# One more weight slot in an expert ring, and a reordered end of the routing, in a two-layer mixture-of-experts kernel

## The reference

```
def hier_moe(h, w_rg, b_rg, w_re, b_re, w_gate, w_up, w_down):
    x = h.reshape(-1, d)
    pg = softmax(x @ w_rg + b_rg)                       # 4 groups
    g_idx, g_prob = argmax(pg), max(pg)                 # the one group of a row
    el = (x @ w_re + b_re).reshape(-1, 4, 8)            # 8 experts in each group
    pe = softmax(el[chosen group])
    top_v, top_i = top_k(pe, 2)                         # two experts of a row
    top_v = top_v / sum(top_v)
    for every expert (g, e):
        hh = silu(x @ w_gate[g, e]) * (x @ w_up[g, e]) * gate[:, g, e]
        y = y + hh @ w_down[g, e]
    ...
hp = hp + yp                                            # mixer A in layer 0, B in layer 1
hp = hp + hier_moe(rms_norm(hp, norm_ffn[i]), ...)
```

## Time and profile before

| | |
|---|---|
| median of 3 runs | 1138.5 us (1138.3 to 1140.09) |
| the profiled execution | 1136.48 us, of which the span of the core's instructions is 1134.6 us |
| PE busy | 1009.6 us (89%), mean granted clock 0.952 |
| DVE, ACT, POOL busy | 421.5, 231.9, 254.0 us |
| DMA | 282.12 MB, mean 249 GB/s; in the expert stages about 417 GB/s |
| expert stage of layer 0 | from 253 us (first gather) to about 485 us |
| expert stage of layer 1 | from 866 us to about 1107 us |

### The profile page before, as it was taken

One profiled execution on the slowest core, in us unless ns is written; L12 is line 12 of the kernel. 1 busy time (PEld: TensorE's weight loads), 2 busy tenths in 40 slices (PEclk: granted clock), 3 DMA queues, 4 the chain that ended last, 5 costly groups with the idle time before them and its releaser, 6 DMA issues.

```text
span 1134.6 us, 17373 instructions
## 1 busy us (share of the span) xinstructions
PE 1009.6 (89%) x6608; PEld 715.2 (63%) x6608; DVE 421.5 (37%) x1367; ACT 231.9 (20%) x717; POOL 254.0 (22%) x408
## 2 busy tenths in 40 slices
PE   6999999978999989839899899999996999888980
PEld 5877777965555545438668687777895555555540
DVE  1234454342333322241242433435464333432326
ACT  4234442110000000033222332332311000000002
POOL 3612232011222221122121221212211122221223
PEclk9999999978999999969999999999996999999995
DMA  9412141569999999993320402227066999999996
GB/s 314 124 40 75 39 186 64 217 244 336 416 419 417 416 420 418 392 317 126 119 80 27 134 31 94 66 102 290 24 258 237 382 419 417 418 418 419 418 372 243
DMA packets 73333, 282.12 MB, mean 249 GB/s; under 512 B 10410, under 2 KB 37114, under 8 KB 47200
## 3 DMA queue, kind: packets, MB, share of 16 engines
q1 hardware_dynamic: 57520, 240.40, 53.9%
q0 software_dynamic: 14480, 31.65, 8.0%
q10 hardware_dynamic: 1248, 8.91, 2.0%
HBM read 268.66 MB, written 28.70 MB: 262 GB/s over the span
## 4 chain that ended last, share of the span: by engine, by line
PE 77%; DMA 13%; DVE 4%; issue 2%; ACT 2%; POOL 1%; SPq 1%; POOLq 0%; ACTq 0%; DVEq 0%
PE ps L1773 22%; PE ps L2075 16%; PE ps L1765 11%; DMA area<-in_w_up 8%; PE ps L2087 7%; PE ps L2060 2%; PE ps L2266 2%; PE ps L1749 2%; PE ps L2082 2%; PE ps L1836 2%; PE ps L1958 1%; PE ps L2232 1%; PE ps L1973 1%; PE ps L1988 1%; DMA area<-y_scratch 1%
## 5 line engine op out<-in xcount | busy, mean ns | idle before, releaser
L1773 PE MATMUL ps<-area 128*128 128x256 f32 x1152 | 266.4, 384 | 7.1 <-DMA area<-in_w_b_qkv 3.3
L2076 PE MATMUL ps<-area 128*64 128x256 f32 x1040 | 251.8, 398 | 0.0
L1773 PEld LDWEIGHTS ps<-area 128*128 128x128 f32 x1152 | 214.0, 191 | 37.9 <-issue 8.2
L2075 PE MATMUL ps<-area 128*64 128x256 f32 x912 | 220.7, 397 | 14.7 <-DMA area<-in_w_up 7.7
L2075 PEld LDWEIGHTS ps<-area 128*64 128x64 f32 x912 | 125.5, 143 | 80.2 <-issue 21.1
L2076 PEld LDWEIGHTS ps<-area 128*64 128x64 f32 x1040 | 143.0, 143 | 0.0
L675 POOL DMA_INDIRECT y_scratch<-area,idx_i x64 | 63.8, 997 | 352.2 <-DVE area L1490 302.3
L1765 PE MATMUL ps<-area 128*128 128x272 f32 x512 | 123.2, 395 | 0.0
L1475 DVE SCALAR_TENSOR_TENSOR area<-ps,area 64x256 f32<-64x256 f32 x64 | 31.4, 491 | 232.4 <-ACT area L966 232.4
L966 ACT ACTIVATE area<-ps,area 64x256 f32<-64x256 f32 x64 | 29.9, 468 | 412.5 <-PE ps L2076 412.5
L2087 PE MATMUL ps<-area 128*64 128x512 f32 x228 | 108.7, 599 | 1.1 <-DVE area L1483 0.8
(11 more groups left out here) (235 smaller groups left out, 1163.6 us busy)
## 6 DMA issues: line engine op xcount, KB each, us to landing
area<-in_w_up SPq DMA_DIRECT2D x65, 1024.0 KB, 24.6
area<-in_w_gate SPq DMA_DIRECT2D x57, 1024.0 KB, 23.0
area<-in_w_down SPq DMA_DIRECT2D x57, 1024.0 KB, 27.4
area<-in_w_b_qkv SPq DMA_DIRECT2D x12, 1024.0 KB, 8.5
hid<-in_w_down SPq DMA_DIRECT2D x8, 1024.0 KB, 24.5
hid<-in_w_gate SPq DMA_DIRECT2D x8, 1024.0 KB, 20.8
area<-y_scratch ACTq DMA_DIRECT2D x8, 1024.0 KB, 8.1
area<-in_w_a_qkv SPq DMA_DIRECT2D x6, 1024.0 KB, 13.0
```

Of the source, the lines that this page charges most:

```text
L1773: ins = nc.tensor.matmul(ps[:r, bank, at_col:at_col + F], x[:, k, COL[t]:COL[t] + r], w[:, k, :], start=k == k0, stop=k == k1 - 1)
L2075: nc.tensor.matmul(ps[0:CAP, bank, 0:F], x[:, k, :], wg[:, k, :], start=k == 0, stop=k == KD - 1)
L2076: ins = nc.tensor.matmul(ps[CAP:P, bank, 0:F], x[:, k, :], wu[:, k, :], start=k == 0, stop=k == KD - 1)
```

## The change

1. The ring has 22 slots in a new order. The new slot, M, lies where the routing's selection matrices are; it stands behind H1 and ahead of H0. It waits for the end of the mixer, for lists and counts (`r_slots`), and for a new semaphore `asked`, which POOL raises right behind the issue of gather 0. H1's wait for the landing of the gather is gone.
2. With the ring, the overfull block moves from expert 20 to expert 22 and its weights from load 64 to load 70.
3. `route_counts` takes three products (ones on `sofar`, ones on the last tile's two `hot`) in place of ten, and runs behind the last `route_slots`; it raises `r_slots` once more, and DVE waits for that ahead of `cnt`.
4. `route_before` does the product on `sofar` first and waits for `hot` only then.
5. The two copies of indices in `route_pick` are gone; the uint32 index is the scalar operand itself.
6. The routing's small tiles lie elsewhere; the overfull block's selection matrices have memory of their own. For a second and later overfull block a wait of DVE stands one step earlier.

```diff
-OV_AFTER = 20
+OV_AFTER = 22
...
-MOE_SLOTS = [["N0", "R4", "R5", "S0", "N1", "F5", "F6", "F0", "F1", "F2", "F3", "F4", "W0", "R0", "R1", "R2", "R3", "X0", "X1", "H1", "H0"]] * 2
+MOE_SLOTS = [["N0", "N1", "F5", "F6", "R4", "R5", "S0", "F0", "F1", "F2", "F3", "F4", "W0", "R0", "R1", "R2", "R3", "X0", "X1", "H1", "M", "H0"]] * 2
...
-    slot_at["S0"], slot_at["W0"] = R_S, 4864
+    slot_at["S0"], slot_at["W0"], slot_at["M"] = R_S, 4864, 6960
...
+        if name == "M":
+            return [(at[c, "o"], UNITS), (r_slots, 2 * layer + 2)]
...
-                    if name == "H1":
-                        sp.wait_ge(gath[0], 16 * (TWOS // XG * layer + 1))
+                    if name == "M":
+                        sp.wait_ge(asked, layer + 1)
                     load(key)
...
-            for j in range(XG):
+            gather(0)
+            pool.sem_inc(asked, 1)
+            for j in range(1, XG):
                 gather(j)
...
-                own(dve, nc.vector.tensor_copy(chosen[:r, t, 0:1], first_of[:r, t, 0, 0:1]))
-                own(dve, nc.vector.tensor_scalar(pen[:r, t, :], iota_e[:r, 0:G], chosen[:r, t, 0:1], -BIG,
+                own(dve, nc.vector.tensor_scalar(pen[:r, t, :], iota_e[:r, 0:G], first_of[:r, t, 0, 0:1], -BIG,
                                                  ALU.not_equal, ALU.mult))
...
-                own(dve, nc.vector.tensor_copy(chosen[:r, t, 1:3], first_of[:r, t, 1, 0:2]))
                 for c in range(2):
-                    ins = nc.vector.tensor_scalar(hot[c][:r, t, :], iota_e[:r, :], chosen[:r, t, 1 + c:2 + c], None,
+                    ins = nc.vector.tensor_scalar(hot[c][:r, t, :], iota_e[:r, :], first_of[:r, t, 1, c:c + 1], None,
                                                   ALU.is_equal)
...
-            dve.wait_ge(r_slots, layer + 1)
+            dve.wait_ge(r_slots, 2 * layer + 1)
...
+            dve.wait_ge(r_slots, 2 * layer + 2)
             own(dve, nc.vector.tensor_scalar(cnt, ps[0:1, 5, 0:NE], float(-CAP), None, ALU.add))
...
-            pe.wait_ge(r_hot, NT * layer + i + 1)
...
-            for c in range(2):
-                ins = nc.tensor.matmul(ps[:r, 4, 0:NE], before[:r, :r], hot[c][:r, t, :], start=c == 0, stop=c == 1 and i == 0)
             if i:
                 pe.wait_ge(r_sum, (NT - 1) * layer + i)
-                ins = nc.tensor.matmul(ps[:r, 4, 0:NE], ones[:, :r], sofar[:, i - 1, :], start=False, stop=True)
+                nc.tensor.matmul(ps[:r, 4, 0:NE], ones[:, :r], sofar[:, i - 1, :], start=True, stop=False)
+            pe.wait_ge(r_hot, NT * layer + i + 1)
+            for c in range(2):
+                ins = nc.tensor.matmul(ps[:r, 4, 0:NE], before[:r, :r], hot[c][:r, t, :], start=c == 0 and i == 0, stop=c == 1)
             ins.then_inc(r_before, 1)
...
         def route_counts(layer):
-            for i, t in enumerate(LATE):
-                r = ROWS[t]
-                for c in range(2):
-                    nc.tensor.matmul(ps[0:1, 5, 0:NE], ones[:r, 0:1], hot[c][:r, t, :], start=i == 0 and c == 0,
-                                           stop=i == NT - 1 and c == 1)
+            t = LATE[NT - 1]
+            nc.tensor.matmul(ps[0:1, 5, 0:NE], ones[:, 0:1], sofar[:, NT - 2, :], start=True, stop=False)
+            for c in range(2):
+                ins = nc.tensor.matmul(ps[0:1, 5, 0:NE], ones[:ROWS[t], 0:1], hot[c][:ROWS[t], t, :], start=False, stop=c == 1)
+            ins.then_inc(r_slots, 1)
...
         route_before(0, 4)
+        route_slots(0, 4)
         route_counts(0)
-        route_slots(0, 4)
```

More of the change, by code:

```diff
@@ L326, in program @@
     y2b = [part(2 * D * i, 2, D) for i in range(3)] + [part(R_X + 2 * D * i, 2, D) for i in range(2)]
[L327 to L334, removed]
-    hot = [h[:, :, 0:NE] for h in hot2]
[L336 to L350, removed]
+    assert 6 * D <= slot_at["M"] and 4 * D <= KD * N
+    R_T = 7232
+    sel = [part(R_T + 640 * i, NT, P) for i in range(2)]
+    both, sofar, em = (part(R_T + 1280 + 160 * i, NT, NE) for i in range(3))
+    stage_g, stage_e = part(R_T, 2, KD, G), part(R_T + 64, 2, KD, NE)
+    R_P = slot_at["M"] + SLOT
+    assert 6208 + 1024 <= R_T and R_T + 1280 + 3 * 160 <= R_P
+    hot2 = [part(R_P + 320 * i, NT, 2 * NE) for i in range(2)]
+    hot = [h[:, :, 0:NE] for h in hot2]
+    lg = part(R_P + 640, NT, NL)
+    gtop, etop = part(R_P + 840, NT, 8), part(R_P + 880, NT, 8)
+    where = part(R_P + 940, NT, 2)
+    pen = part(R_P + 950, NT, G)
+    rs = part(R_P + 970, 12, 8)
+    gexp = part(R_P + 1066, NT, G)
+    gw = part(R_P + 1086, 2, 8)
+    ovs = part(R_P + 1102, 128)
+    shifted = part(R_P + 1230, NT, 2)
+    root = part(R_P + 1240, NE)
+    idx_f = part(R_P + 1272, NE)
+    assert R_P + 1304 <= R_G
+    blocks = part(R_X + 2 * SLOT, NE * 8)
+    ov_at = [R_G + P * i for i in range(8)] + [R_F + 7 * SLOT + P * i for i in range(2)]
+    ov_sel = [[part(ov_at[NT * c + t], P) for t in range(NT)] for c in range(2)]
     first_of = sb("first_of", [P, NT, 2, 8], U32)
@@ L405, in program @@
     r_clear = sem("r_clear")
+    asked = sem("asked")
     ones = cst[:, C_ONE:C_ONE + P]
@@ L1430, in moe @@
             ins.then_inc(r_idx, 1)
-            own(dve, nc.vector.tensor_scalar(em[:, 0, :], ps[:, 3, 0:NE], -2.0, float(2 * KEY0), ALU.mult, ALU.add))
-            nc.vector.tensor_scalar(idx_i[:, 0, :], em[:, 0, :], cst[:, C_HALF:C_HALF + 1], None, ALU.add) \
+            own(dve, nc.vector.tensor_scalar(idx_f, ps[:, 3, 0:NE], -2.0, float(2 * KEY0), ALU.mult, ALU.add))
+            nc.vector.tensor_scalar(idx_i[:, 0, :], idx_f, cst[:, C_HALF:C_HALF + 1], None, ALU.add) \
                 .then_inc(r_idx, 1)
@@ L1523, in overfull_select @@
                     for c in range(2):
-                        ins = nc.vector.tensor_scalar(sel[c][:r, t, :].rearrange("p (a b) -> p a b", b=CAP), slot_no[:r], shifted[:r, t, c:c + 1],
+                        ins = nc.vector.tensor_scalar(ov_sel[c][t][:r, :].rearrange("p (a b) -> p a b", b=CAP), slot_no[:r], shifted[:r, t, c:c + 1],
                                                       cst[:r, (C_K1, C_K2)[c] + t:(C_K1, C_K2)[c] + t + 1],
@@ L1581, in moe @@
                     overfull_pick(o)
+                    wait_apart(dve, s["scat"], 16 * o)
                     overfull_select(o)
-                    wait_apart(dve, s["scat"], 16 * o)
                     overfull_rows(o)
@@ L2116, in overfull_list @@
                     for c in range(2):
-                        ins = nc.tensor.matmul(ps[:, 3, 0:2 * NE], sel[c][:r, t, :], hot2[c][:r, t, :],
+                        ins = nc.tensor.matmul(ps[:, 3, 0:2 * NE], ov_sel[c][t][:r, :], hot2[c][:r, t, :],
                                                start=t == 0 and c == 0, stop=t == NT - 1 and c == 1)
@@ L2334, in _ @@
         route_before(1, 4)
+        route_slots(1, 4)
         route_counts(1)
-        route_slots(1, 4)
         moe(1)
```

## The result

The changed kernel takes 1145.2 us (median) where the kernel before takes 1138.6: ratio 1.0047, 95% interval [1.0033, 1.0062]. It is slower by 5.4 us by the ratio (3.8 to 7.1) and by 6.6 between the medians; 4.1 us less were forecast, and 1137.7 was the upper end of the range. The profiled execution of after took 1145.5 us, with a span of 1143.7, 9.1 us more than the one of before. That is more than the ratio says, because the profiled execution of before (1136.48 us) was faster than each of the 13 runs of before, and that of after was close to the median.

What follows compares the result with a forecast made beforehand. Weight traffic was taken to bound layer 0, PE layer 1. Layer 0: 2.5 + 0.96 - 0.3 = 3.2; layer 1: 0.96 - 1.1 + 1.0 = 0.9; together 4.1 us off, median 1134.4 us, range 1130.3 to 1137.7.

Steps and rivals of the forecast that it cites:

- when `asked` comes: Start of layer 0's experts: the semaphore rises after POOL's 1.31 us for gather 0, at 254.6 less the routing's gain.
- what the first gather pays: Start of each expert stage: gather 0 lands later beside H1, by 0.3 us in layer 0 and 1.1 in layer 1.
- M's data come behind the gather's: Start of layer 0's experts: M's traffic follows gather 0's; 0.3 us (0 to 2.2) was taken for the gather's delay.
- they hardly meet: Start of layer 0's experts: H1's traffic, to about 254.5, and gather 0's data scarcely overlap; 0.3 us taken.
- The prediction's own sign of being wrong: Start of the expert stages: the prediction is wrong if gather 0 takes above 6 us.
- PE's start is late by the whole of it: Start of each expert stage, claimed if gather 0 takes 9.3 us: PE starts 4.3 us late in each layer.
- rival 3: First gather, both layers: it takes the later gathers' 9.3 us; together 5.1 us slower, 1143.6 us; chance 0.07.
- here it is one: First gather: the 9.3 us median stands behind some ten loads in the queue, here behind only one.
- the slot: Weight queue: 22 loads in before the first refill; layer 0 2.5 us earlier, layer 1 nothing in the time.
- the routing: Mixer's end, last tile: copies gone, products reordered; 0.96 us less for each layer, bounds 0.39 and 0.96.
- the block: Layer 1's overfull block: PE's stall of 2.3 us shrinks by 1.0, DVE's copy next late; bounds 0 and 2.3.
- The clock: After layer 1's block stall: granted clock 0.70 over 5.7 us, a loss of 1.7; gain counted 0, upper bound 1.7.

Runs made afterwards that it cites:

- run 2: The changed kernel with `asked` raised by a small POOL memset behind gather 0 instead of a plain increment; ratio 0.9972 [0.9951, 0.9993] to the kernel before.
- run 1: The changed kernel with M (and H0 behind it) held until gather 0 has landed, H1 still early; ratio 0.9973 [0.9954, 0.9993] to before, median 1138.8 us.
- the kernel of 3: The changed kernel with H1, M and H0 all behind gather 0's landing; ratio 0.9938 [0.9915, 0.9960] to before, 0.9958 in a repeat.
- run 5: The kernel before with the overfull block alone moved from expert 20 to 22, ring of 21; ratio 1.0002 [0.9983, 1.0021] to before.

## Why the prediction was wrong, step by step

- **Failed: when `asked` comes.** "Gather 0 is issued at 253.28 and takes POOL 1.31 us, so `asked` comes at 254.6." The sum laid the increment behind the gather's 1.31 us because it stands there in the program. In after it is done 0.24 us before they begin (252.50 against 252.74), and M is asked for ahead of the gather in both layers. Run 2 puts the increment about where the sum had it: the gathers fall from 9.71 and 9.55 us to 6.84 and 8.39.
- **Mis-sized: what the first gather pays.** 0.3 and 1.1 us were taken, 5.7 and 5.4 measured, 5.4 and 4.3 us too little; together that is more than twice the whole forecast gain. "M's data come behind the gather's" failed with the increment, and run 2 shows that it would have failed in part even without that: M and H0, asked for behind POOL's work, still cost 1.4 and 2.1 us. H1's own term was too small too: even with M behind the landing it is 1.45 and 2.1 (run 1), and in layer 0 "they hardly meet" was wrong. H1 leaves at 247.25 and lands at 256.1, 3.4 us after POOL began on the gather. The prediction's own sign of being wrong, gather 0 above 6 us, was right.
- **Held: PE's start is late by the whole of it**, and layer 0's full queue hides nothing, since the first refill waits for expert 0 (271.32 against 265.52). It was rival 3's mechanism: a gather that takes 9.3 us in both layers and 1143.6 us; measured 9.7, 9.6 and 1145.2. It got a chance of 0.07 because "here it is one" load; it is two, with a third just behind, and the gather takes what the median takes.
- **Held: the slot.** From the first refill's issue to the landing of the last up matrix of layer 0: 472.78 - 265.52 = 207.3 us before, 208.0 in the kernel with 21 slots and the new routing, 204.3 in after (475.6 - 271.3) and in the kernel of 3. That is 3.0 us; 2.5 were forecast from the load's size. The last up load of after and its landing:

```profile
L520 SPq DMA_DIRECT2D area<-in_w_up x1: 2737/2737/2737, 446.6 to 446.6; - x1
...
DMA to landing us min/median/max: 29.0/29.0/29.0
```

- **Held: the routing**, 0.96 us forecast for each layer, 0.94 and 0.94 measured in its own run from the end of the logits to POOL's start on the gather; in the time of that run 3.5 [1.7, 5.4], whose lower part holds the 1.9. The copies are gone and nothing came in their place; the readers of the uint32 index take what they took before (0.23 us, and 0.39 for the two of `hot`). The wait that is left is in the chain of after as `247.81 1.08 PE ps L1862 x4` and `249.91 1.13 PE ps L1871 x4`, with no count product ahead of the lists.
- **Held in the stall, not in the time: the block.** 2.3 to 1.1 us and DVE's copy as what is late next, but run 5 shows no gain in the time. The clock, for which a gain of 0 was counted with 1.7 as its bound, went the other way in after: from the block's first gate product to the next expert's it takes 12.9 us against 10.6 in before, and that expert's gate and up 5.3 against 3.7, 3.9 us more in all. In the kernel of 3 it is 10.4 and 3.7.
- **The chances.** The slot and the routing came as forecast, the block in its stall only; the sum hung on the gather's term, whose first condition no row of before could show, and its bound for layer 0 (2.2) was taken from a gather behind two loads, not from the median of the full queue, which the prediction had at hand. With 5.3 as the upper bound in both layers the range would have reached 1143.6, still 1.6 us short of the result; the clock at the block, for which no loss was allowed, is larger than that.

## What to carry to other kernels

As these runs show it for a gather of POOL, a semaphore increment that stands behind a DMA's issue in the program says nothing on where the DMA is; what may only follow a transfer must wait for its landing, or stand behind work that shows in the trace (which in run 2 still left 1.4 and 2.1 us of the cost). A small transfer on which everything waits is worth an idle queue: look for the gap behind its landing, and ask for the large ones there, as the kernel of 3 does in the 9 us before the first refill. And when a sum of small gains meets one unknown cost at the head of the chain, bound that cost by the worst row of the same transfer, not by the nearest.

## What was not expected of the hardware

- POOL's sequencer does a plain increment while the gather ahead of it has not begun on the engine: 252.50 against 252.74 to 254.05; a memset with the same increment comes at 253.93, behind it.
- Loads asked for 0.2 us after POOL's work on the gather (254.13 against 253.93) still lengthen it, from 5.4 to 6.8 us and from 6.3 to 8.4; each of these is one trace, and the gathers with nothing ahead of them differ by up to 0.7 from trace to trace.
- The same instructions after the same stall of 1.1 us go on at a mean granted clock of 0.68 in one trace and 0.87 in another; whether the kernel or the execution decides is open.
